# HGRN output norm on 384 columns: one product of ones with the squares, variance and power on full width

## The reference

```python
def rmsnorm(x, g):
    xf = x.astype(jnp.float32)
    y = xf * lax.rsqrt(jnp.mean(xf * xf, axis=-1, keepdims=True) + EPS)
    return y.astype(x.dtype) * g
...
    o = o_f + rev(o_b)                                  # (B, L, heads, 128)
    o = rmsnorm(o, norm_g) * jax.nn.silu(heads(zg))     # mean over a head's 128 values
    return o.reshape(B, L, D_MODEL).astype(h.dtype) @ w_out, ...
```

## Time and profile before

| | us |
|---|---|
| time, median of 3 runs (lowest, highest) | 3049.49 (3047.04, 3051.56) |
| the profiled execution's own time | 3052.63 |
| its span | 3050.7 |
| PE busy | 2975.5 |
| DVE busy | 2204.6 |
| ACT busy | 1155.3 |
| POOL busy | 582.9 |

### The profile page before, as it was taken

One profiled execution on the slowest core, in us unless ns is written; L12 is line 12 of the kernel. 1 busy time (PEld: TensorE's weight loads), 2 busy tenths in 40 slices (PEclk: granted clock), 3 DMA queues, 4 the chain that ended last, 5 costly groups with the idle time before them and its releaser, 6 DMA issues. The chain is left out here.

```text
span 3050.7 us, 46591 instructions
## 1 busy us (share of the span) xinstructions
PE 2975.5 (98%) x18382; PEld 2759.2 (90%) x18382; DVE 2204.6 (72%) x2845; ACT 1155.3 (38%) x1967; POOL 582.9 (19%) x586
## 2 busy tenths in 40 slices
PE   6999999999999999999999999999999999999999
PEld 6989888999999998999999989979999999888998
DVE  5888677887887566888888576658778888775444
ACT  4222564222422434222422265543224222564222
POOL 1111212112211202112211144441112112211001
PEclk9999999999999999999999999999999999999999
DMA  8676535666566355766566433337665666334443
GB/s 294 199 227 190 142 74 175 209 210 200 173 213 186 99 152 149 224 207 208 187 210 200 135 109 98 98 94 225 211 210 161 216 212 202 116 70 126 127 125 97
DMA packets 565933, 515.58 MB, mean 169 GB/s; under 512 B 43013, under 2 KB 499286, under 8 KB 563926
## 3 DMA queue, kind: packets, MB, share of 16 engines
q1 hardware_dynamic: 565158, 512.37, 55.3%
q10 hardware_dynamic: 560, 0.25, 0.0%
HBM read 509.31 MB, written 3.24 MB: 168 GB/s over the span
## 5 line engine op out<-in xcount | busy, mean ns | idle before, releaser
L1618 PE MATMUL bank<-h_hi,w_hi 128*128 128x384 f32 x3328 | 1122.5, 337 | 5.3 <-DVE tmp L2073 2.7
L1620 PE MATMUL bank<-h_hi,w_lo 128*128 128x384 f32 x3328 | 1116.3, 335 | 0.0
L1619 PE MATMUL bank<-h_lo,w_hi 128*128 128x384 f32 x3328 | 1115.0, 335 | 0.0
L1865 ACT ACTIVATE w_hi<-raw 128x1024 fp32r<-128x1024 f32 x648 | 682.6, 1062 | 1084.1 <-PE bank L1620 450.7
L2021 DVE TENSOR_TENSOR w_lo<-raw,w_hi 128x1024 fp32r<-128x1024 f32 x648 | 809.2, 1271 | 343.6 <-ACT w_hi L1865 339.1
L2043 DVE SCALAR_TENSOR_TENSOR fold<-ada_raw,cond,fold 128x1024 f32<-128x1024 f32 x476 | 654.5, 1432 | 0.0
L1618 PEld LDWEIGHTS bank<-h_hi,w_hi 128*128 128x128 f32 x3328 | 626.4, 188 | 16.8 <-ACT tmp L1884 3.4
L1619 PEld LDWEIGHTS bank<-h_lo,w_hi 128*128 128x128 f32 x3328 | 626.4, 188 | 6.0
L1620 PEld LDWEIGHTS bank<-h_hi,w_lo 128*128 128x128 f32 x3328 | 626.1, 188 | 0.0
L2330 POOL TENSOR_TENSOR h_lo<-tmp,h_hi 128x384 fp32r<-128x384 f32 x176 | 281.5, 1600 | 1760.3 <-DVE h_hi L2077 1760.3
L1665 PE MATMUL bank<-w_hi,h_hi 128*128 128x512 f32 x1056 | 416.1, 394 | 0.0
(11 more groups left out here) (199 smaller groups left out, 2416.8 us busy)
## 6 DMA issues: line engine op xcount, KB each, us to landing
raw<-w_ffn_in SPq DMA_DIRECT2D x352, 512.0 KB, 5.0
ada_raw<-w_ada SPq DMA_DIRECT2D x272, 512.0 KB, 4.2
raw<-w_ffn_out SPq DMA_DIRECT2D x176, 512.0 KB, 4.7
raw<-w_hgrn_in SPq DMA_DIRECT2D x40, 512.0 KB, 3.9
g_rows<-g_dram SPq DMA_DIRECT2D x12, 1024.0 KB, 6.6
raw<-w_attn_qkv SPq DMA_DIRECT2D x24, 512.0 KB, 5.8
raw<-w_conv_in SPq DMA_DIRECT2D x24, 512.0 KB, 4.9
ada_first<-w_ada SPq DMA_DIRECT2D x16, 512.0 KB, 12.5
```

The source lines that it names most:

```text
L1618: mm(out, wh, h_hi[:, k, :], start=(k == 0), stop=False)
L1619: mm(out, wh, h_lo[:, k, :], start=False, stop=False)
L1620: last = mm(out, wl, h_hi[:, k, :], start=False, stop=(k == DC - 1))
L1865: A(w_hi[:, b % RING, :], raw[:, b % RAW, :], ACT.Copy).then_inc(w_hi_made, 1)
```

## The change

PE multiplies a 128x128 tile of ones with the squares (`norm_sums`, now one 384-column product a head in step 0): the sums of all tokens come out on every partition at once. The variance is computed on 128x384 from the bank into `hg_v`, the power is taken on 128x384 in place on POOL, now behind its level 1, and `norm_output` multiplies `tmp` by it, now in step 3. The diagonal and the spreading product are gone. High and low part come one step (level) later.

```diff
@@ pe_hgrn
         def norm_sums(z, i):
 
             pe.wait_ge(o_gated[z], i + 1)
-            for t in range(NT):
-                last = mm(psum[OUT + z][:, T + t:T + t + 1], hg_q[:, 2 * i + z, t * P:(t + 1) * P], ones[:, 0:1],
-                          start=True, stop=True)
-            last.then_inc(o_var[z], 1)
-
-        def norm_spread(z, i):
-
-            pe.wait_ge(o_dg_made[z], i + 1)
-            mm(psum[OUT + z][:, 0:T], ones[:, :], hg_v[:, 2 * i + z, :], start=True, stop=True).then_inc(o_spread[z], 1)
+            mm(psum[OUT + z][:, 0:T], ones[:, :], hg_q[:, 2 * i + z, :], start=True, stop=True).then_inc(o_var[z], 1)
...
-                elif k == 2 and i > 0:
-                    norm_spread(z, i - 1)
...
-                elif c == 1:
-                    norm_spread(z, last_pair)
@@ act_hgrn
-                elif k == 3 and i > 0:
+                elif k == 4 and i > 0:
                     high_part(z, i - 1)
@@ dve_hgrn
             dve.wait_ge(o_var[z], i + 1)
-            V.tensor_scalar(hg_r[z][:, 0:NT], psum[OUT + z][:, T:T + NT], 1.0 / P, EPS, ALU.mult,
+            V.tensor_scalar(hg_v[:, 2 * i + z, :], psum[OUT + z][:, 0:T], 1.0 / P, EPS, ALU.mult,
                             ALU.add).then_inc(var_read[z], 1)
 
-        def norm_diagonal(z, i):
+        def norm_output(z, i):
 
             dve.wait_ge(root_made[z], i + 1)
-            V.tensor_tensor(hg_v[:, 2 * i + z, :].rearrange("p (t q) -> p t q", t=NT),
-                            ident.unsqueeze(1).to_broadcast([P, NT, P]),
-                            hg_r[z][:, 4:4 + NT].unsqueeze(2).to_broadcast([P, NT, P]),
-                            ALU.mult).then_inc(o_dg_made[z], 1)
-
-        def norm_output(z, i):
-
-            dve.wait_ge(o_spread[z], i + 1)
             dve.wait_ge(o_gated[z], i + 1)
-            V.tensor_tensor(tmp[:, 2 + z, :], psum[OUT + z][:, 0:T], tmp[:, 2 + z, :], ALU.mult).then_inc(o_step[z], 1)
+            V.tensor_tensor(tmp[:, 2 + z, :], hg_v[:, 2 * i + z, :], tmp[:, 2 + z, :], ALU.mult).then_inc(o_step[z], 1)
...
-                if k == 1 and i > 0:
-                    norm_diagonal(z, i - 1)
-                elif k == LEVELS:
+                if k == LEVELS:
                     far(z, i)
...
-                elif k == 2 and i > 0:
+                elif k == 3 and i > 0:
                     norm_output(z, i - 1)
@@ gp_hgrn_core
             gp.wait_ge(var_read[z], i + 1)
-            G.tensor_tensor(hg_r[z][:, 4:4 + NT], hg_r[z][:, 0:NT], m_half, ALU.pow).then_inc(root_made[z], 1)
+            v = hg_v[:, 2 * i + z, :]
+            G.tensor_tensor(v, v, m_half[:, 0:1].to_broadcast([P, T]), ALU.pow).then_inc(root_made[z], 1)
...
-                    if lv == 0 and i > 0:
+                    if lv == 1 and i > 0:
                         norm_root(z, i - 1)
-                    elif lv == 3 and i > 0:
+                    elif lv == 4 and i > 0:
                         low_part(z, i - 1)
```

More of the change, by code:

```diff
@@ L421, in build @@
     lb_exp = put("lb_exp", [P, DIRS, DEPTH, HG])
-    hg_r = [put(f"hg_r{z}", [P, 8]) for z in range(2)]
     hg_low = [put(f"hg_low{z}", [P, NT, 32]) for z in range(2)]
@@ L477, in build @@
         per_slot("kr_turned"), per_slot("kt_copied"), per_slot("st_done"), per_slot("st_copied"))
-    o_dg_made, o_spread = per_slot("o_dg_made"), per_slot("o_spread")
     o_done, o2_made, o_var, var_read, root_made, o_step = (
@@ L1425, in dve_hgrn @@
             step(last_pair, k)
-        for make in (norm_variance, norm_diagonal, norm_output):
+        for make in (norm_variance, norm_output):
             for z in range(2):
```

## The result

The changed kernel takes 3530.23 us as the median of 4 runs (3527.91 to 3532.91), the kernel before 3048.26 beside it: ratio 1.158, 95% interval 1.156 to 1.159. Forecast was 3508.5. The profiled execution has a span of 3530.9 us against 3050.7, 480.2 more.

What follows compares the result with a forecast made beforehand. TensorE, busy 98%, was taken to bound the kernel. Three pairs' waits (334.5), the mixer's end (108.3) and low clock (16) add 459 us to the profiled 3052.63, giving 3508.5 us for the median; range 3190 to 3545.

Steps and rivals of the forecast that it cites:

- one power of 384 columns: POOL's wide power: 57.8 us, from the slope of 149.5 ns a column between one and three columns.
- slots 1 and 2: First two pairs' powers, done in the next pair's steps: PE's level 3 comes 111.5 us late each, plus clock.
- third slot: Third pair's powers, done in the last pair's steps: priced like the other slots, 111.5 us plus 4 us of clock.
- end of the mixer: Last pair's powers: PE gets its output block 108.3 us late, behind output, high part and both weight splits.
- low clock after a wait: PE at half clock after each of four long waits: 4 us each, 16 us in all, bounds 0 and 6 each.
- cover: Part of two powers not delaying PE: 4.1 us in pairs 1 to 3 (115.6 less 111.5), 7.3 at the end.
- sum, in the span: Three pairs' waits 334.5, the end 108.3 and clock 16: 459 us added.
- first rival: POOL's power runs two or three times as fast per column in long rows: 3281 or 3205 us; chance 0.17.
- second rival: PE does other work during the waits, so only the last pair may fill its wait: 3396 us; chance 0.03.
- third rival: POOL's wide power costs as the subtraction does, 1.25 us, and nothing waits: 3044 us, 0.18% faster; chance 0.12.
- turning point: Power of about 2.1 us on POOL, half of the cover; beyond it each microsecond of power costs eight.
- PE's saving: One-column products removed from PE: 1.36 us less a pair, -5.4 us in all, swallowed by the waits.

Runs made afterwards that it cites:

- the law of the price: Changed kernel with the power on only the first 12 (pow_12) or 128 (pow_128) of 384 columns: 3050.43 us and 3203.63 us.
- wide_mult: Changed kernel with POOL multiplying the 128x384 variances by -0.5 instead of raising them to that power: 3046.96 us, ratio 0.9994.
- pow_12: Changed kernel with the power on only the first 12 of the 384 columns: 3050.43 us, ratio 1.0007.
- the pair of single-slot kernels: Changed kernel with the 384-column power for only the first or only the third pair, 3 columns elsewhere: 3172.96 us and 3164.45 us.

## Why the prediction was right, step by step

| step | forecast us | measured us |
|---|---|---|
| one power of 384 columns | 57.8 | 61.52 |
| slots 1 and 2, a pair (clock in it) | 115.5 | 121.6, 121.5 |
| the same with a power of 61.52 | 122.9 | 121.6, 121.5 |
| third slot, with a power of 61.52 | 122.9 | 117.5 |
| end of the mixer, with a power of 61.52 | 119.7 | 119.7 |
| low clock after a wait | 4 | 2.8 in slots 1 and 2, 3.0 at the end |
| cover, slot 1 | 4.1 | 4.3 |
| sum, in the span | 459 | 480.2 |

The measured slots are the distances of the starts less those of before; the third is 151.79 - 39.98 = 111.8 plus the 5.7 us by which the first powers start later (1870.46 against 1864.79), a lead that the end takes back. The end is what is left of 480.2.

**Price.** The mechanism held and the term was mis-sized: 3.7 us a power, 29.8 us for eight. With it alone the forecast would have been 489, 8 too much. The slope came from one and three columns, and the shortest row does not lie on the line of the long ones. The first rival (a cheaper loop in long rows) is excluded by the law of the price, the third by the same. What took the 8 us back was the clock (1.4 us in each of two slots) and the third slot (5.4 us), both below.

**Place.** The three waits at the level products, released through ScalarE, and the fourth behind VectorE's split are where they were put. That the last wait ends with the weight split and not with the low part was found by following what stands in line behind the waiting output on VectorE and ScalarE; the path behind the second power was 3.5 us by forecast and 4.2 in the trace. The second rival is excluded too: PE did nothing during the waits.

**Cover.** The size held, in part by luck. The cover is how much of two powers does not show as a delay of level 3 against the kernel before, whose own window is

```profile
1864.79:1924.56 59.77, 58.51 (x726) 1.00 0.34 98
```

There PE waits 1.3 us and has 1.2 us more of work than wide_mult. In the changed kernel waiting grew to 121.2 us, by 119.9, and 1.2 us of work went: 118.7 us of delay for 123.05 us of power, 4.3 hidden. pow_12 gives 4.1 (1.6 us more waiting than before, 1.2 less work, 4.53 us of power). The parts of my sum were less good: POOL's level 1 took 4.7 us (1865.73 to 1870.46), not 4.0, and behind the powers the first head's keys took 1.3 us (0.34 + 1.04, overlapping) where I had 2.05 from the earlier trace rows. The two errors cancel. For the third rival the turning point of 2.1 us a power thus stands by the waits; pow_12 at 2.27 us a power is 1.9 us a pair behind before (61.71 against 59.77), of which 1.5 is the half clock behind its waits, a term that I had not put into the turning point.

**PE's saving.** 1.36 us of work a pair by forecast was 1.16 in the busy time and 1.07 in the starts (58.70 against 59.77), and wide_mult as a whole is not measurably faster (0.15% at most by its interval). My 3044 us for the third rival was 3 us too hopeful.

**Clock.** The fall to half clock came behind each long wait, but it was over-sized: 2.8 us in slots 1 and 2 and not 4. With the measured price and this clock the forecast of these slots is 121.7, against 121.6 and 121.5 measured. At the end it cost 3.0. In the third slot I counted wait and clock beside waits and a low stretch that the kernel before has in that very place. That is the larger part of the 5.4 us by which the third slot came out below; the pair of single-slot kernels shows 5.9 us between the slots, 3.8 of waits and 2.1 of clock.

## What to carry to other kernels

Take the root where each value exists once. After the product with a full tile of ones all 128 partitions hold the same 384 numbers, and the power is paid 128 times over; three columns cost 0.86 us, and the diagonal and the second product that spread them are cheaper than 61.5 us of power by far. When an operation is widened, look for two rows of it at different widths and take the slope, not the rate of another operation of the same shape; when a pair grows by as much as an operation did, divide the growth into waiting and busy time before calling it cover, as part of it can be the clock; and when it goes into an in-order queue, price everything queued behind it, up to the engine that waits last.

## What the runs showed that I had not expected

- The power on POOL is a line in the columns, 360 + 159.2 ns each from 12 to 384, the same within 27 ns over eight instances (61514 to 61541). In the first three pairs VectorE worked for 3.1 us beside the first power and not at all beside the second, so this says little on contention. A multiplication of the same shape takes 824 ns, 75 times less.
- A short key update of POOL (L1427, 128x96) took 0.34 us with VectorE waiting (changed and pow_12), and 0.46 to 0.93 beside VectorE's work (before and wide_mult). No run changes VectorE's work alone, so that it is the cause is not shown.
- Two waits of 1.06 and 0.92 us close together were followed by about 4 us at half clock (pow_12); a wait of 0.56 us was not (wide_mult). But in the kernel before the granted clock also fell to 0.50 for some 3.3 us (about 1981.0 to 1984.3), with no wait longer than 0.43 us ahead of it in that pair; what decides on such a short fall stays open.
- VectorE's output multiplication, now with both operands in SBUF, took 0.54 us in the pairs, as with one operand in the bank, but 1.18 us beside the second head's power and 1.34 us beside POOL's low part at the mixer's end. Both of these also followed 60 us of waiting, and no run tells the two apart.
- VectorE's reciprocal of 128x384 takes 2532 ns.
